# Two blocks of a transformer on one core: where the last head steps of an attention group stand in the order of work

## What is computed

```
q, kc, vc, ks, vs, kw, vw, gl = split(rmsnorm(x) @ w_in)        # 16 heads in 4 groups of 4
kcc, vcc = compress(kc), compress(vc)                            # 15 compressed keys per group
o_c = softmax(q @ kcc.T + bias_c) @ vcc                          # compressed branch
o_s = softmax(q @ ks.T + bias) @ vs                              # selected blocks (all 4 are selected)
o_w = softmax(q @ kw.T + bias) @ vw                              # window
h   = x + (g0 * o_c + g1 * o_s + g2 * o_w) @ w_out
```

## Time and profile before

| | |
|---|---|
| median of 3 runs | 2103.74 us (2103.24 to 2103.88) |
| span of the profiled execution | 2103.4 us |
| TensorE busy | 2084.6 us, 99% |
| VectorE busy | 1508.8 us, 72% |
| ScalarE busy | 1059.9 us, 50% |
| granted TensorE clock | 0.999 on average |

### The profile page before, as it was taken

The page is one execution under the profiler, slowest core; times in us unless marked ns, Lnnn a source line. Parts: engine busy times, 40 slices in busy tenths (PEclk is TensorE's granted clock), DMA queues, the critical chain, the costliest instruction groups (busy, mean ns, idle before and its releaser), DMA issues.

```text
span 2103.4 us, 29344 instructions
## 1 busy us (share of the span) xinstructions
PE 2084.6 (99%) x11460; PEld 1791.6 (85%) x11460; DVE 1508.8 (72%) x1998; ACT 1059.9 (50%) x1529; POOL 21.8 (1%) x41
## 2 busy tenths in 40 slices
PE   9999999999999999999999999999999999999998
PEld 8888888888888888888888888888888888888887
DVE  6868666788889888988766767577555555556555
ACT  6654555554444434444456666465443444344443
POOL 0000000000000000000000000000000000000000
PEclk9999999999999999999999999999999999999999
DMA  8787334788898999988765525455555555555553
GB/s 333 272 314 281 104 118 162 283 325 323 324 339 325 365 371 346 344 325 336 303 263 172 212 86 189 182 217 194 195 187 196 186 198 188 192 193 187 198 182 121
DMA packets 74968, 506.40 MB, mean 241 GB/s; under 512 B 8730, under 2 KB 9226, under 8 KB 16976
## 3 DMA queue, kind: packets, MB, share of 16 engines
q1 hardware_dynamic: 70992, 488.67, 63.4%
q0 software_dynamic: 3120, 15.07, 1.9%
q10 hardware_dynamic: 720, 0.79, 0.1%
HBM read 501.79 MB, written 2.18 MB: 240 GB/s over the span
## 4 chain that ended last, share of the span: by engine, by line
PE 94%; DVE 3%; ACT 2%; issue 1%; DMA 0%; DVEq 0%; ACTq 0%; SPq 0%
PE region L1163 40%; PE region L1097 30%; PE region L1101 16%; PE region L1152 2%; PE region L1153 1%; ACT m_SP L1623 1%; PE bank L1260 1%; PE bank L1136 1%; DVE m_WLO L1930 1%; PE bank L1219 1%; ACT m_WHI L1543 1%; PE bank L1209 1%; DVE m_SP L2090 1%; PE bank L1273 1%; PE bank L1188 0%
## 5 line engine op out<-in xcount | busy, mean ns | idle before, releaser
L1930 DVE TENSOR_TENSOR m_WLO<-m_RAW,m_WHI 128x1024 fp32r<-128x1024 f32 (+3 forms) x729 | 867.6, 1204 | 476.8 <-ACT m_WHI L1543 451.9
L1543 ACT ACTIVATE m_WHI<-m_RAW 128x1024 fp32r<-128x1024 f32 (+3 forms) x729 | 752.9, 1042 | 655.3 <-PE region L1163 308.9
L1163 PE MATMUL region<-m_WHI,m_HL 128*128 128x512 f32 x1152 | 359.9, 394 | 0.1
L1097 PE MATMUL region<-m_HL,m_WHI 128*128 128x512 f32 x1472 | 357.5, 393 | 0.0
L1097 PE MATMUL region<-m_H,m_WHI 128*128 128x512 f32 x1376 | 328.7, 391 | 0.0
L1097 PEld LDWEIGHTS region<-m_HL,m_WHI 128*128 128x128 f32 x1472 | 269.6, 188 | 52.1 <-issue 0.3
L1097 PEld LDWEIGHTS region<-m_H,m_WHI 128*128 128x128 f32 x1376 | 252.9, 188 | 48.9
L1163 PEld LDWEIGHTS region<-m_WHI,m_HL 128*128 128x128 f32 x1152 | 213.0, 188 | 43.5 <-issue 1.3
L1966 DVE CUSTOM_DVE_ANT_0 m_RAW<-m_RAW,m_CROW,m_consts 128x2048 f32<-128x2048 f32 x96 | 225.1, 2345 | 0.0
L1163 PE MATMUL region<-m_WLO,m_HL 128*128 128x512 f32 x576 | 224.5, 390 | 0.0
L1163 PE MATMUL region<-m_WLO,m_HIDH 128*128 128x512 f32 (+1 forms) x512 | 198.3, 387 | 0.0
(11 more groups left out here) (338 smaller groups left out, 1733.6 us busy)
## 6 DMA issues: line engine op xcount, KB each, us to landing
m_RAW<-in_w_ff SPq DMA_DIRECT2D x124, 1024.0 KB, 4.8
m_RAW<-in_w_mod SPq DMA_DIRECT2D x96, 1024.0 KB, 6.6
m_RAW<-in_ffn_w_in SPq DMA_DIRECT2D x88, 1024.0 KB, 6.0
m_RAW<-in_ffn_w_out SPq DMA_DIRECT2D x44, 1024.0 KB, 6.8
m_RAW<-in_nsa_w_in SPq DMA_DIRECT2D x36, 1024.0 KB, 6.7
m_RAW<-in_nsa_w_out SPq DMA_DIRECT2D x16, 1024.0 KB, 4.9
m_RAW<-in_w_out SPq DMA_DIRECT2D x16, 1024.0 KB, 4.8
m_RAW<-in_w_first SPq DMA_DIRECT2D x8, 1024.0 KB, 5.2
```

The lines of the kernel that those rows point to most:

```text
L1097: mm = e.matmul(region[s["reg"]][:, b, :], hi[:, i, c:c + 128], both[:, k + a + i, :, :].rearrange("p a s -> p (a s)"), start=k + a + i == ...
L1163: mm = e.matmul(o, lhs, rhs, start=start and i == 0, stop=fin and i == 2, skip_group_check=True)
L1543: e.activation(WHI[u % 4][:, 0:(z - a) * ncol], raw[:, a * ncol:z * ncol], ACT.Copy).then_inc(a_hi, 1)
L1930: e.tensor_tensor(WLO[u % 4][:, 0:m], raw[:, a * ncol:z * ncol], WHI[u % 4][:, 0:m].bitcast(F32), ALU.subtract).then_inc(v_lo, 1)
```

## The change

The first edit stands beside the second query slab: q0 adds 0.75 of a credit per chunk as before, q1 only 0.25. By the credits one modulation product fewer is put at the end of q1; every later product moves one place down the list, and a place that was empty at the end of the feed-forward layer takes the last one.

The second edit is in the queue of head steps. At the first head i of groups 1, 2 and 3 (i = 4, 8, 12) the steps now come in this order: `soft3` i-1 and `turn` i-2,0; `values` i-3 and `out` i-3; `turn` i-2,1; `cscore` g; two times nothing (four times in group 3); `cturn` g; `scores` i and `soft1` i; `soft2` i. Before, it was: nothing; `cscore` g; four times nothing; `cturn` g; `soft3` i-1 and `turn` i-2,0; `scores` i and `soft1` i; `turn` i-2,1 and `soft2` i; `values` i-3 and `out` i-3. The remaining three heads of a group keep their order. Groups 1 and 2 have 21 places where they had 23.

Counting ticks, which are the same before and after (21 steps in q4 and q5, 21 in q6 and q7), the list on TensorE reads as follows. A bar is a place where a tick stands, W, L and T are matmuls of a slab or a tile of `out1`; `soft1`, `soft2`, `soft3` and `out` go with their steps.

The diff:

```diff
--- before.py
+++ after.py
@@ -619,7 +619,9 @@
     run(nsa["vs"], nsa["gl"], nsa["vw"])
     side.extend([("kcc",), ("vcc",), *[u for g in range(4) for u in (("vput", g), None)]])
     st["gemv"] = 0.75
-    run(*nsa["q"][0:2])
+    run(nsa["q"][0])
+    st["gemv"] = 0.25
+    run(nsa["q"][1])
     drain()
 
 
@@ -652,6 +654,17 @@
     def tiles(x, k):
         return [k] if x == "h2" or k < 8 else [2 * k - 8, 2 * k - 7]
 
+    def keep_or_put(k, at, x):
+
+        own = tiles(x, k)
+        if st["parts"] >= hl_free(x, own[0]):
+            flush(x)
+            st["puts"] += 1
+            P.put_no[at + k] = st["puts"]
+            have[x] = own[-1] + 1
+        else:
+            got[x] += own
+
     def attention(at, lo, n, last, x, since=0):
 
         for i in range(lo, n + 3 if last else n):
@@ -667,6 +680,26 @@
                 if i < n:
                     unit("scores", at + i)
                     put("soft1", at + i)
+            if 0 < at + i < 16 and i % 4 == 0:
+                g = i // 4
+
+                def s4(i=i):
+                    unit("turn", i - 2, 1)
+
+                def s5(i=i):
+                    unit("scores", i)
+                    put("soft1", i)
+
+                def s7(i=i):
+                    put("soft2", i)
+
+                def s6(i=i):
+                    unit("values", i - 3)
+                    put("out", i - 3)
+                    keep_or_put(i - 3, at, x)
+                side.extend([s6, s4, lambda g=g: unit("cscore", g), *[None] * (2 if g < 3 else 4),
+                             lambda g=g: unit("cturn", g), s5, s7])
+                continue
             if at + i == 24 and i < n:
                 side.extend([lambda: put("rope", 0), None, None, s1])
             elif at + i == 25 and i < n:
@@ -689,19 +722,13 @@
                     k = i - 3
                     if at + k == 27:
                         put("warm", 1)
-                    own = tiles(x, k)
-                    if st["parts"] >= hl_free(x, own[0]):
-                        flush(x)
-                        st["puts"] += 1
-                        P.put_no[at + k] = st["puts"]
-                        have[x] = own[-1] + 1
-                    else:
-                        got[x] += own
+                    keep_or_put(k, at, x)
                 side.append(s3)
 
     st["rate"], st["gemv"] = 1.3, 0.0
     for g in range(4):
-        side.extend([None] * (1 if g else 2) + [("cscore", g)] + [None] * 4 + [("cturn", g)])
+        if g == 0:
+            side.extend([None] * 2 + [("cscore", g)] + [None] * 4 + [("cturn", g)])
         attention(0, 4 * g, 4 * g + 4, g == 3, "h2")
         if g < 3:
             run(*nsa["q"][2 * g + 2:2 * g + 4])
```

## The result

The changed kernel takes **2110.86 us** (median of 5 runs, 2109.96 to 2112.45), the one before 2103.88 us (5 runs, 2103.24 to 2104.35) on the same chip: ratio 1.0032, 95% interval 1.0021 to 1.0043. It is slower by 7.0 us. The forecast was 2107.8 us with a range up to 2109.4; the result lies 1.5 us above it. The forecast also held the two most likely (0.58) to be less than 4.2 us apart. The profiled execution took 2109.96 us, with a span of 2108.2 us.

What follows compares the result with a forecast made beforehand. TensorE, busy 2084.6 of 2103.4 us, was taken as the bound, so only its waits could move. Terms -0.6 - 1.5 + 1.0 + 0.3 + 0.4 + 4.8 - 0.3 = +4.1 gave 2107.8 us, range 2102.8 to 2109.4.

Steps and rivals of the forecast that it cites:

- Product: Beside q1: without the product the chain of `cscore` 0 begins sooner and `cturn` 0's wait goes, -0.6 us (-0.6 to 0).
- cscore 1: Two places later: its wait goes, -1.5 us; then `values` 1 waits +1.0 for bank 7, `cscore` 1 +0.3 for bank 6.
- cturn 1, 2 and 3: Turns behind `cscore`: 1 and 2 lose cover but cost 0; 3 loses its shorter wait, -0.3 us.
- soft2 ahead of evac: ScalarE, end of q4 and q6: exponentials ahead of `evac` make everything behind it 1.4 us late (0 to 1.8).
- q7 and out1: q7 and first tiles of `out1`: waits up to `values` 9 for bank 7, +4.8 us (3.2 to 5.2), 3.2 at `values` 9.
- rival 3: Clock falls in the long wait, matmuls behind it at the lower level for 3 to 10 us: 2111 to 2118, chance 0.06.
- Rival 2: Backlog goes on into `out1`, heads 10 to 12 wait 1 us each for bank 7 or 6: about 2111, chance 0.07.
- rival 1: Bank 7 is in time in q7, so `values` 9 doesn't wait: 2100.8 to 2103.0 us, chance 0.17.
- turn 3,1: In q4/q5: this `turn` waits because `evac`, split and copy end late, +0.4 us (0 to 0.8).
- Places where a step interrupts the matmuls: Two more in the slabs, three fewer in `out1`: ±0.25 us, taken as 0.
- The base: Whole run: the sum was put on the span of 2103.4 us, with the median 0.3 above that span.

Runs made afterwards that it cites:

- e1: Kernel before with the first edit alone (0.25 of a credit in place of 0.75 beside q1): 2103.81 us, ratio 0.9998.
- e6: Changed kernel with head 8's exponentials (`soft2` 8) moved behind the `evac` of q6: 2108.52 us, ratio 1.0021.
- e4: Changed kernel with twelve unused matmuls of ones put in front of `values` 9: 2108.66 us, ratio 1.0021.
- e5: Changed kernel with the new order in group 1 only, groups 2 and 3 in the order of before: 2103.64 us, ratio 0.9998.
- e7: Kernel before with the product edit and another list for group 1, `cscore` 1 late and `values` 1 behind it: 2102.67 us, ratio 0.9993.
- e3: Changed kernel with group 3's steps back in the old order: 2109.81 us, ratio 1.0027.
- e8: Changed kernel with group 3 in the old order and eight unused matmuls of ones ahead of `cscore` 3: 2108.52 us, ratio 1.0020.
- e9: Changed kernel with `values` 9 moved behind `cscore` 3, two tiles of `out1` later: 2105.57 us, ratio 1.0006.
- e10: Changed kernel with `values` 1 and `values` 9 behind their `cscore` and head 8's exponentials behind q6's `evac`: 2103.00 us, ratio 0.9994.
- e2: Changed kernel without the first edit, so only the new order of head steps: 2110.24 us, ratio 1.0031.

## Why the prediction was wrong

**The steps that held.** *Product*: -0.6 forecast, 0.6 of wait gone and -0.75 in the stage of e1. *cscore 1*: -1.5, all gone; `values` 1 waits 0.85 for 1.0, `cscore` 1 behind it 0.40 for 0.3. *cturn 1, 2 and 3*: no wait. *soft2 ahead of evac*: `evac` starts 277.38 - 275.47 = 1.9 us after the slab's end, forecast were 1.6 to 1.7; e6 shows that this is the exponentials. *q7 and out1*: the old list, read with each head one higher, gave a `turn` 8,1 without its margin, 1.4 us at `turn` 9,1 and 3.2 at `values` 9; they are 0.73, 1.36 and 3.10, and `turn` 7,1 has 0.23. The term was +4.8; these four are 5.4, less the 0.8 of before +4.6.

**The step that failed: rival 3 and its chance.** The clock fell behind the 3.1 us wait. I gave that 0.06, with a price of 3 to 10 us (+7 to +14 with the 4.1 of the sum), because I supposed 3 to 10 us of work at the lower level; no row stood behind these bounds. Both were wrong, in opposite directions: a mean clock with a fall in it shows in 14 of 20 executions with that wait, and the fall costs 1.5 us in the profiled execution and 2.2 in the medians (changed kernel against e4). A first price had its row: one `values` of 1.65 us right behind the wait at half speed is +1.65. How long the clock stays low beyond it stood in no row. The Trainium skill, "TensorE: Matmul & The Clock Gate", section "Why this matters for your kernels", which tells to keep idle gaps between bursts of matmuls short, spoke against the forecast. I had set it aside because no row of before shows such a gap. This trace agrees with it, by the granted clock of 0.50 from 306 to 308 behind the 3.10 us of idle time. A new wait of twice the longest in the trace is no case for the trace's "the clock is 1.00 throughout": that row speaks for waits up to 1.5 us and says nothing beyond. With the fall in the forecast, 2107.8 + 1.5 to 2.2 is 2109.3 to 2110.0, 0.9 to 1.6 under the result.

**The other rivals.** Rival 2, a backlog of 1 us waits in heads 10 to 12, had a time of about 2111, which the result nearly meets. That is chance: behind the wait of `values` 9 TensorE waits nowhere up to 1000. In rival 1 the low end of 2100.8 doesn't follow from its terms, 2103.7 - 2.4 - 0.8 + 0.9 is 2101.4; nothing else hung on it.

**turn 3,1, +0.4.** It does not wait, and e5 has no `turn` wait in q4 and q5 either. This error is in the other direction; why the later `evac` leaves no wait there stays open.

**Places where a step interrupts the matmuls, taken as 0 with ±0.25.** Take the change of the waits from the change of the stage: for e1, e5 and e7 the rest is within 0.2 us. For the changed kernel, without the 1.5 us of clock, it is +0.6, and for e3, e4, e8, e9 and e10, all with group 2's new list and no fall of the clock, +0.4 to +0.9 (the fillers of e4 and e8 counted as the waits that they fill). e2 and e6, less 1.6 and 1.8 us for their slowed rows, have +0.8 and +0.4. Some half a microsecond stands in no wait and was outside my bound. That it comes with group 2's list is shown; where it lies, and whether it is the interruptions, isn't.

**The base.** I put the median 0.3 above the span. All executions on record lie 1.8 or 1.9 us above their spans (changed: 2109.96 and 2108.2), so the profiled execution of before, with 2103.4, was itself longer than the median by 1.3 us. The number hardly suffered: 2107.8 is also the median plus 4.1. The reason given for it was wrong.

**The sum again.** e4 has all waits of the forecast and no fall: +4.15 in the stage, +4.4 in the medians, for +4.1. The changed kernel has 7.0. The 2.6 us between them are 2.2 from the changed kernel's median to e4's and 0.4 between the medians of before beside each. Of the 2.2 the profiled executions show 1.5 as clock. The other 0.7 isn't traced to a cause: the profiled execution of the changed kernel is the fastest of its five, 0.9 us under their median, one of the five has a mean clock of 0.997, and medians of five and eleven runs leave some tenths uncertain.

## What to carry to other kernels

Read the old trace as the forecast of the new list, with each step in its new place, and take the waits from where each bank comes free: this gave the three largest new waits (3.10, 1.36 and 0.85 us) to 0.2 us. Then look at the longest new wait by itself. If it is longer than any wait of the trace, the granted clock of the trace proves nothing for it, and the work right behind it at half speed is the least price to book. And before a change of order is given up, move the one waiting step behind work that waits for nothing: one step moved took back 4.3 of 5.6 us, while returning the whole group to its old order took back 2.1.

## What the runs showed of the hardware

One idle stretch of 3.1 us on TensorE, in a stage where it is otherwise busy, was followed by a granted clock of 0.50 from 306 to 308 in each of the three profiled executions that have it (changed, e2, e6). With the same wait filled by matmuls of ones (2.84 us busy, 0.41 idle) the clock stayed at 1.00. The mean clocks of all executions, which don't say where the clock fell, are under 0.999 in 14 of 20 with that wait and in 0 of 11 with it filled; with a longest wait of 1.95 us in 2 of 7, with waits of 1.5 us and less in 0 of 148 (83 of before, 65 of e1, e5, e7, e8, e9 and e10). The DMA engines stood nearly still in the same wait, a share of 0.00 to 0.01 from 300 to 306. That the loads wait for buffers which TensorE's progress frees would explain this; it wasn't tried.
